# Prompt attention of a two-path decoder step: other column groups for the weighted sum, and another order on ScalarE

## The reference, cut to what matters

```python
s = einsum('bqhd,bkhd->bhqk', q, k) / sqrt(HEAD_DIM)
s = where(k_pos <= q_pos, s + cq[..., :, None] - ck[..., None, :], -inf)
p = softmax(s, axis=-1)
o = einsum('bhqk,bkhd->bqhd', p, v)          # then h = h + o @ w_o, and a squared-ReLU MLP
```

## Time and profile before

| | us |
|---|---|
| median of 3 runs | 2298.28 (2297.35 to 2299.89) |
| the profiled execution, its own time | 2298.19 |
| its span in the profile | 2296.3 |
| PE busy, PEld busy | 2271.3 (99%), 2085.1 (91%) |
| DVE, ACT, POOL busy | 1037.9, 579.0, 614.0 |
| first scores of the prompt attention to the first matmul of the output projection | 1182.90 to 1453.72 |

### The profile page before, as it was taken

How to read it: one execution, slowest core, us unless ns; L and a number is a source line. 1 busy time by engine, 2 the same in 40 slices (tenths; PEclk the granted TensorE clock), 3 DMA queues, 4 the chain that set the end, 5 groups by cost and what they waited for, 6 DMA issues and landing times.

```text
span 2296.3 us, 36346 instructions
## 1 busy us (share of the span) xinstructions
PE 2271.3 (99%) x14226; PEld 2085.1 (91%) x14226; DVE 1037.9 (45%) x1758; ACT 579.0 (25%) x1264; POOL 614.0 (27%) x445
## 2 busy tenths in 40 slices
PE   8999999999999999999999999999999999999999
PEld 8999999999999977777776666899999999999999
DVE  7842332433423766542147878434433423324332
ACT  6420110110101443332136777322110101101101
POOL 6222222222222622100001112353333323323340
PEclk9999999999999999999999999999999999999999
DMA  5111111111111124444564644111111111111112
GB/s 153 41 46 47 47 47 47 47 46 47 47 47 47 56 92 148 138 133 146 182 179 104 137 108 102 37 46 47 47 47 47 47 47 47 47 47 47 47 56 76
DMA packets 195560, 169.96 MB, mean 74 GB/s; under 512 B 28784, under 2 KB 169120, under 8 KB 195399
## 3 DMA queue, kind: packets, MB, share of 16 engines
q1 hardware_dynamic: 155493, 141.50, 21.5%
q10 hardware_dynamic: 39914, 26.23, 3.7%
HBM read 137.55 MB, written 30.50 MB: 73 GB/s over the span
## 4 chain that ended last, share of the span: by engine, by line
PE 92%; DVE 4%; ACT 2%; issue 1%; DMA 0%; DVEq 0%; ACTq 0%
PE ps L366 35%; PE ps L631 29%; PE ps L821 13%; PE ps L1593 4%; PE ps L493 2%; PE ps L1554 2%; PE ps L1569 2%; PE ps L1555 1%; ACT pT L1639 1%; DVE tmp_b L443 1%; PE ps L837 1%; PE ps L1315 1%; PE ps L1836 1%; PE ps L1295 1%; PE ps L1337 1%
## 5 line engine op out<-in xcount | busy, mean ns | idle before, releaser
L366 PE MATMUL ps<-xn_hi,w_lo 128*128 128x352 f32 x1528 | 494.9, 324 | 4.3 <-DVE h L709 3.5
L366 PE MATMUL ps<-xn_lo,w_hi 128*128 128x352 f32 x1528 | 489.8, 321 | 0.0
L366 PE MATMUL ps<-xn_hi,w_hi 128*128 128x352 f32 x1528 | 489.5, 320 | 0.0
L631 PE MATMUL ps<-hid_hi,w_lo 128*128 128x352 f32 x1440 | 464.5, 323 | 0.0
L631 PE MATMUL ps<-hid_lo,w_hi 128*128 128x352 f32 x1440 | 461.9, 321 | 0.0
L631 PE MATMUL ps<-hid_hi,w_hi 128*128 128x352 f32 x1440 | 461.4, 320 | 0.0
L333 POOL CAST w_hi<-w_raw 128x1024 fp32r<-128x1024 f32 x132 | 138.8, 1052 | 994.8 <-issue 506.0
L709 DVE TENSOR_TENSOR h<-ps,h 128x352 f32<-128x352 f32 x360 | 185.9, 522 | 413.0 <-PE ps L631 413.0
L670 ACT ACTIVATE tmp_b<-tmp_a 128x352 f32<-128x352 f32 x192 | 95.0, 499 | 1076.0 <-DVE tmp_a L692 1076.0
L335 POOL TENSOR_TENSOR w_lo<-w_raw,w_hi 128x1024 fp32r<-128x1024 f32 x132 | 319.1, 2418 | 10.6
L366 PEld LDWEIGHTS ps<-xn_hi,w_lo 128*128 128x128 f32 x1528 | 286.6, 188 | 7.2 <-DVE h L709 4.7
(11 more groups left out here) (254 smaller groups left out, 2730.5 us busy)
## 6 DMA issues: line engine op xcount, KB each, us to landing
w_raw<-in_w_up SPq DMA_DIRECT2D x64, 512.0 KB, 4.0
w_raw<-in_w_down SPq DMA_DIRECT2D x60, 512.0 KB, 3.4
out<-tok_out ACTq DMA_DIRECT2D x32, 256.0 KB, 2.2
qk_dram<-turn_hi ACTq DMA_DIRECT2D x32, 256.0 KB, 2.4
qk_dram<-turn_lo ACTq DMA_DIRECT2D x32, 256.0 KB, 2.9
k_page<-in_cache_k SPq DMA_DIRECT2D x32, 256.0 KB, 3.4
v_page<-in_cache_v SPq DMA_DIRECT2D x16, 512.0 KB, 9.3
q_a<-qk_dram SPq DMA_DIRECT2D x32, 256.0 KB
```

The source lines that it names most:

```text
L366: last = pe.matmul(ps[:, bank, 0:CH], w, x(k, c), start=(k == 0 and i == 0), stop=(k == nk - 1 and i == 2))
L631: last = pe.matmul(ps[:, NC * (dm % 2) + c, 0:CH], w, x, start=(k == 0 and i == 0), stop=(k == GT - 1 and i == 2))
```

## The change

`weigh` now takes a range of key blocks, and its two column groups hold other query blocks of the four in the group: partitions 0 to 63 take the first and the last (`0:4:3`), partitions 64 to 127 the two in the middle. Where a key block meets the diagonal (d = kb - 4g above 0), each column group multiplies only the query blocks that still see it. There are three pieces a head: group 0 whole at slot 4, and group 1 of the head before in two pieces of four key blocks at slots 0 and 2. VectorE's `out` waits for the whole group and stands at slots 1 (group 0) and 3 (group 1) of the next head, where it stood at slots 6 and 4. On ScalarE `exp(n + 3)` now stands ahead of `turned(n)`.

```diff
-                for kb in range(kb0, kb0 + 2):
-                    lo = max(0, kb - 4 * g) * P
-                    for q in range(2):
-                        c = max(lo - 256 * q, 0)
-                        if c < 256:
-                            last = pe.matmul(ps[HD * q:HD * q + HD, 6 + av % 2, c:256], v_h[hh % 2][:, kb, :],
-                                             pT[g][:, kb, 256 * q + c:256 * q + 256],
-                                             start=(kb == 0), stop=(kb == 4 * g + 1 + 2 * q))
-                            if kb >= 4 * g and kb == 4 * g + 1 + 2 * q:
-                                last.then_inc(o_full, 1)
+                for kb in range(kb0, kb1):
+                    x = pT[g][:, kb, :].rearrange("p (r c) -> p r c", c=P)
+                    d, v, bank = kb - 4 * g, v_h[hh % 2][:, kb, :], 6 + av % 2
+                    if d <= 0:
+                        pe.matmul(ps[0:HD, bank, 0:2 * P], v, x[:, 0:4:3, :], start=(kb == 0), stop=False)
+                    else:
+                        outer = pe.matmul(ps[0:HD, bank, P:2 * P], v, x[:, 3, :], start=False, stop=(d == 3))
+                    if d <= 1:
+                        pe.matmul(ps[HD:P, bank, 0:2 * P], v, x[:, 1:3, :], start=(kb == 0), stop=False)
+                    elif d == 2:
+                        pe.matmul(ps[HD:P, bank, P:2 * P], v, x[:, 2, :], start=False, stop=True).then_inc(o_full, 1)
+                    else:
+                        outer.then_inc(o_full, 1)
...
-                if n % NQ in (4, 5):
-                    weigh(n - n % 4 - 1, 2 * (n % 4))
-                elif n % NQ < 4 and n >= NQ:
-                    weigh(n - n % 4 - 1, 2 * (n % 4))
+                if n % NQ == 4:
+                    weigh(n - 1, 0, 4)
+                elif n % NQ in (0, 2) and n >= NQ:
+                    weigh(n - n % NQ - 1, 2 * (n % NQ), 2 * (n % NQ) + 4)
...
-            for kb0 in range(0, NQ, 2):
-                weigh(NBLK - 1, kb0)
+            weigh(NBLK - 1, 0, NQ)
...
-                turned(n)
                 if n + 3 < NBLK:
                     exp(n + 3)
+                turned(n)
...
-                for q in range(2):
-                    dve.wait_ge(o_full, 2 * av + q + 1)
-                    c = 512 * g + 256 * q
-                    dve.tensor_copy(oT[HD * e:HD * e + HD, hh // 2, c:c + 256],
-                                    ps[HD * q:HD * q + HD, 6 + av % 2, 0:256]).then_inc(o_ev, 1)
+                dve.wait_ge(o_full, 2 * av + 2)
...
-                if n % NQ == 6:
+                if n in (NQ + 6, NBLK - 2):
                     out(n - 3)
-                elif n % NQ == 4 and n > NQ:
-                    out(n - 5)
+                elif n % NQ == 1 and n > NQ and n != 2 * NQ + 1:
+                    out(n - 6)
+                elif n % NQ == 3 and n > NQ:
+                    out(n - 4)
```

More of the change, by code:

```diff
@@ L1571, in turn, with weigh @@
                     last.then_inc(t_full, 1)
-            def weigh(n, kb0):
+            def weigh(n, kb0, kb1):
                 hh, g = n // NQ, n // 4 % 2
@@ L1667, in out @@
                 e, av = hh % 2, 2 * hh + g
-                for q in range(2):
-                    dve.wait_ge(o_full, 2 * av + q + 1)
-                    c = 512 * g + 256 * q
-                    dve.tensor_copy(oT[HD * e:HD * e + HD, hh // 2, c:c + 256],
-                                    ps[HD * q:HD * q + HD, 6 + av % 2, 0:256]).then_inc(o_ev, 1)
+                dve.wait_ge(o_full, 2 * av + 2)
+                rows = oT[HD * e:HD * e + HD, hh // 2, 512 * g:512 * g + 512].rearrange("p (r c) -> p r c", c=P)
+                for q, dst in ((1, rows[:, 1:3, :]), (0, rows[:, 0:4:3, :])):
+                    dve.tensor_copy(dst, ps[HD * q:HD * q + HD, 6 + av % 2, 0:2 * P].rearrange("p (r c) -> p r c",
+                                                                                          c=P)).then_inc(o_ev, 1)
             top(0)
```

## The result

The changed kernel takes 2326.4 us (2323.42 to 2328.08, 4 runs), the one before, measured beside it, 2299.09 us: 1.0117 times as long, 95% interval 1.0104 to 1.0129. It is 27 us slower. I had forecast 2312, with a range up to 2324: the right side and the right place, but half the size (13 us of 27).

A forecast was written before the change was run, and what follows sets the result against it. TensorE's own queue was taken to set the pace. Heads 1 to 14 at +0.82 us (11.5), head 0 +1.5 and the last +0.5 made +13.5 on 2298.19: 2312 us, own range 2305 to 2320, widened to 2290 to 2324.

The forecast's parts named there:

- B, A and C: The new weigh pieces on TensorE: slot 0 (key blocks 0 to 3) 1.88 us, slot 4 1.24, slot 2 1.24.
- the 0.17 that goes with a piece: TensorE's step from the last transpose to weigh, saved with each piece that goes: three steps of 0.17 us a head.
- lock step: Rival: TensorE's column groups keep strict order, +0.21 us a head, 2315 us; its chance lies within the chain's 0.72.
- the stops stay as they are: Rival: TensorE's stops do not grow, a head takes 13.93 or 14.67 us, kernel faster at 2276 us; chance 0.14.
- the two runs of 128: TensorE's moving operand read as two runs of 128: priced 0, bounds -0.02 and +0.1 us a piece.
- From B to the scores of slot 3: TensorE's stretch from a head's first weigh to block 6's scores: 5.50 us before, -0.11 after.
- from there to the second quad of block 4: TensorE from block 6's scores, through maximum, exponential and block 3's copy, to block 4's fifth transpose: 4.26 us, 3.89 before.
- The stop inside block 4: TensorE waits 1.34 us before the second quad of block 4's five transposes; expected sign 1.2 to 1.5 us.
- From there to block 6's: From block 5's transposes to block 6's: four transposes, a hand-over, ScalarE's copy and a hand-over, 1.38 us.
- the step before: From block 4's second quad, through block 7's exponential and a copy, to block 5's transposes: 2.15 us.
- no one on the path waits for them: Semaphores, SP's value loads and GpSimd's cuts, released within 5 us of where they were: priced at 0.
- a rival of mine at 4%: The clock: TensorE's stops bring half clock in a sixth of the stage, about 40 us, 2352 us; chance 0.04.

The follow-up runs named there:

- experiment 1: The changed kernel with ScalarE's old order (a block's copies ahead of the exponential of three blocks on): 2287.11 us, 0.9943 of before.
- experiment 5: Changed kernel with ScalarE's old order, GpSimd's second-half cut held until the next head's slot 0, output-projection splits moved behind earlier cuts: 2281.42 us, 0.9916 of before.
- experiment 2: The kernel before with only ScalarE's new order, its six pieces and unequal groups kept: 2332.62 us, 1.0143 of before.
- experiment 8: The changed kernel with ScalarE's new order kept in slots 0 to 2 and the old one in slots 3 to 7: 2286.43 us, 0.9940 of before.
- experiment 3: The changed kernel with only block 5's copies put ahead of the exponential of block 0 of the next head: 2315.75 us, 1.0065 of before.
- experiment 4: The changed kernel with GpSimd's cut of a head pair's second half held back until slot 0 of the next head: 2323.26 us, 1.0097 of before.

## Why the prediction was right and wrong, step by step

**Right: the pieces.** B, A and C, the 0.17 that goes with a piece, lock step excluded, the clock at 1.00 beside the stops of ordinary heads. My time for the rival "the stops stay as they are", 14.67 us a head, is what the odd heads of experiments 1 and 5 take. The extra passes and the two runs of 128 cost nothing that shows. The Trainium skill says that matmuls stay monotone in start and end (TensorE: Matmul & The Clock Gate, The mechanism; I had named the section behind it). The trace of C differs: the first group starts its fourth step at 1324.81 (the second pass of the row at 1324.70), and the second group's last pass, of the third step, starts at 1324.92, though the program has it first.

**Right: the mechanism of the loss, and its main term.** From B to the scores of slot 3 it is 5.36 us (forecast 5.39), from there to the second quad of block 4 4.05 (4.26; block 3's copy is followed within 0.04 and not 0.14, and the maximum starts 0.07 sooner). The stop inside block 4 is 1.14 us where I had 1.34, a little under the 1.2 to 1.5 that I gave as its sign. Experiments 1, 2 and 8 show that ScalarE's order is the cause and slots 3 to 7 the place.

**Wrong: "From there to block 6's: four transposes (0.33 to the last start), 0.31, copy 0.60, 0.14: 1.38."** It takes 2.03 us. The step took the exponential of block 0 as something that stood ready ahead of the copy. Its buffer is the one of block 5, and it waits for all six transposes: 0.55 to the start of the last, 0.39, then 0.36 for itself, then the copy. I had written down just this condition for block 7's exponential on block 4, and had not gone through it for the others; `P_BACK` is 3 for blocks 0, 6 and 7. With +0.12 for the step before and -0.21 from block 4, an odd head is 17.41 us and not 16.92: +0.49, 7 us over 14 heads. Experiment 3 takes the term away: its odd head is 16.80, and the kernel is some 11 us faster.

**Missing: GpSimd.** I priced at 0 that `out`, and with it GpSimd's cut, moved by a slot ("no one on the path waits for them"). No one waits for them, but the subtraction runs beside VectorE's scaling of block 5, which is now on the path: 0.5 us in every second head, 3.5 us in all. Experiments 4 and 5 show it, by holding GpSimd's cut back; `out` itself was not moved back in any run.

**Left out: head 14's splits, and the clock beside them.** GpSimd's splits of 8 us fall in head 14 and make it 19.42 us, 1.5 more than an even head. A part of that is the clock: with stops of 0.6 to 1.1 us in each block TensorE was busy for 1.02 to 1.66 of every 2 us from 1450 to 1458, and it ran at half clock from about 1458 to 1461. It was a rival of mine at 4%, with a far larger price. The splits I had not priced at all. Of the 1.5 us, 1.4 lie from 1457.55 (block 6's transposes) to 1461.73, which takes 4.18 us where an even head takes 2.78; TensorE is busy through it without a stop, and its matmuls follow each other more slowly (block 7's eight transposes and the step behind them take 1.57 us, 0.81 in the odd head). That is not all the clock's price: in experiment 3 the same splits fall in head 14 with the clock at 1.00 and make it 18.17, 0.85 longer than an even head, by a stop before block 7's transposes. The half clock took the place of that stop and left, by this estimate, some 0.6 us on top.

Together, in the profiled executions: from the mask's matmul of block 3 of head 0 to the output projection 267.70 us before (1186.02 to 1453.72) and 293.38 after (1188.06 to 1481.44), +25.7. Head 0 gave +1.7 (forecast 1.5), the last head +0.1 (0.5), heads 1 to 14 +23.9 (11.5), of which 11.5 + 6.9 + 3.5 + 1.5 = 23.4 are named. The remaining 2 us lie ahead of the stage, where the program is the same: in the executions of these kernels its start there varies from 1185.7 to 1191.0 us.

## What to carry to other kernels

An in-order queue that serves two chains should serve first what is ready first. Here, putting the exponential, which was needed later, ahead of a copy that was ready laid the exponential's wait on the copy; and where the exponential's buffer was freed only by the transposes that the copy was to take over (block 5), two hand-overs became one long one. So when an order changes, write down for *each* step, not only for the longest, what it waits for, buffers included. And an instruction moved by one slot moves the engines that it releases; ask also what they disturb, not only who waits for them.

## What I had not expected of the hardware

VectorE's scaling of 128x768 fp32 within SBUF takes 0.62 us alone and 1.21 beside a GpSimd subtraction. The reductions that VectorE reads from PSUM show no such stretch: the one at 1343.96 runs beside GpSimd's cast and the start of its subtraction and takes 1.09, as in the earlier trace rows. The Trainium skill (SBUF — State Buffer, Terms) says that VectorE and GpSimd share a port pair that one of them holds for a whole instruction, while the other is fully blocked. The trace agrees: GpSimd's subtraction ends at 1345.95, and the scaling that was issued at 1345.16 ends 0.42 after it. What is left after GpSimd's end goes by the size of the scaling and not by how long the two overlap: it is 0.15 us for 256 columns (experiment 5, at 1389.67), 0.42 for 768, and 0.48 for 896, both in the kernel before, where the scaling at 1397.05 takes 1.15, and in head 14 of the changed one, where it takes 2.58 (0.69 alone):

```profile
1453.65 2.58 DVE L1666 TENSOR_SCALAR p_lo<-p_lo,stat 128x896 f32<-128x896 f32 x1
```

```profile
1453.39 2.36 POOL L335 TENSOR_TENSOR w_lo<-w_raw,w_hi 128x1024 fp32r<-128x1024 f32 x1
```

Within one piece of column-tiled fp32 matmuls the two column groups need not keep step: in C the first group starts 128-column passes every 0.109 us while the second is in passes of 0.216, and both start their last pass together (1324.92), 1.23 us for 640 columns each.
